# A recurrence on one core: output square sums with the next pair's, transposed values in the solve's first level, one convolution tap a half block later

## What is computed

```python
qkv_a = silu(causal_conv(qkv_a, conv_w))          # 4 taps per channel
q_a = l2norm(q_a) * (GDN_HEAD_DIM ** -0.5);  k_a = l2norm(k_a)
o_a = gated_delta_rule(q_a, k_a, v_a, g, beta)
o_a = rmsnorm(o_a, gdn_norm_w).reshape(b, s, GDN_WIDTH) * silu(z_a)

# gated_delta_rule, by chunks
l_mat = where(strict, einsum("bhncd,bhnjd->bhncj", k_beta, k) * decay, 0.0)
sol = triangular_solve(l_mat + eye, concatenate([v * beta, k_beta * exp(g_cum)], -1))
u, w = sol[..., :dv], sol[..., dv:]
def step(state, inp):
    v_new = u_c - w_c @ state
    o_c = q_c @ state + qk_c @ v_new
    return state * dec_c + k_c.T @ v_new, o_c
```

## Time and profile before

| | us |
|---|---|
| median of 3 runs | 3890.14 (3889.11 to 3890.8) |
| the profiled execution | 3890.46 |
| its span, first to last instruction | 3888.7 |
| TensorE busy | 3736.6 (96%) |
| its weight loads busy | 3492.0 (90%) |
| VectorE busy | 2862.1 (74%) |
| ScalarE busy | 1904.7 (49%) |
| mean granted TensorE clock | 0.993 of full speed |

### The profile page before, as it was taken

The page is one execution under the profiler, slowest core; times in us unless marked ns, Lnnn a source line. Parts: engine busy times, 40 slices in busy tenths (PEclk is TensorE's granted clock), DMA queues, the critical chain, the costliest instruction groups (busy, mean ns, idle before and its releaser), DMA issues.

```text
span 3888.7 us, 70287 instructions
## 1 busy us (share of the span) xinstructions
PE 3736.6 (96%) x27254; PEld 3492.0 (90%) x27254; DVE 2862.1 (74%) x3924; ACT 1904.7 (49%) x2898; POOL 186.9 (5%) x188
## 2 busy tenths in 40 slices
PE   1999999999999999999999999999999999999998
PEld 1999999899988999999989998999987888989888
DVE  8788887867779778888686776665676666666676
ACT  1556565435544355555534554454665433344365
POOL 0111111000000012121000000000000000000000
PEclk8999999999999999999999999999999999999999
DMA  9543443864468844434486445544534445455543
GB/s 394 182 145 142 141 145 135 302 236 164 155 239 317 290 148 141 150 135 151 146 317 214 158 152 182 185 163 172 190 120 149 177 181 188 180 184 184 184 143 128
DMA packets 138699, 720.49 MB, mean 185 GB/s; under 512 B 37696, under 2 KB 38144, under 8 KB 62336
## 3 DMA queue, kind: packets, MB, share of 16 engines
q1 hardware_dynamic: 111456, 631.31, 45.0%
q10 hardware_dynamic: 27040, 86.32, 6.6%
HBM read 711.22 MB, written 2.16 MB: 183 GB/s over the span
## 4 chain that ended last, share of the span: by engine, by line
PE 84%; DVE 7%; ACT 4%; issue 3%; DMA 2%; DVEq 0%; ACTq 0%; SPq 0%
PE bank L300 16%; PE bank L283 13%; PE bank L285 13%; PE bank L284 13%; PE bank L301 8%; PE bank L322 3%; PE bank L2410 2%; PE bank L2412 2%; PE bank L2411 2%; ACT Wh L356 2%; PE bank L326 2%; DMA raw<-in_ada 1%; DVE Wl L362 1%; PE bank L1077 1%; DVE gm_more L1308 1%
## 5 line engine op out<-in xcount | busy, mean ns | idle before, releaser
L356 ACT CAST Wh<-raw 128x1024 fp32r<-128x1024 f32 x1124 | 1168.2, 1047 | 1610.3 <-PE bank L285 913.5
L362 DVE TENSOR_TENSOR Wl<-raw,Wh 128x1024 fp32r<-128x1024 f32 x1124 | 1381.5, 1235 | 692.0 <-ACT Wh L356 688.9
L283 PE MATMUL bank<-H,Wh 128*128 128x256 f32 x4928 | 1445.5, 293 | 2.0 <-DVE Wl L362 1.2
L284 PE MATMUL bank<-H,Wh 128*128 128x256 f32 x4928 | 1393.0, 283 | 0.0
L285 PE MATMUL bank<-H,Wl 128*128 128x256 f32 x4928 | 1392.4, 283 | 0.0
L283 PEld LDWEIGHTS bank<-H,Wh 128*128 128x128 f32 x4928 | 941.6, 191 | 26.1 <-issue 13.6
L284 PEld LDWEIGHTS bank<-H,Wh 128*128 128x128 f32 x4928 | 942.2, 191 | 8.0 <-issue 4.8
L285 PEld LDWEIGHTS bank<-H,Wl 128*128 128x128 f32 x4928 | 941.3, 191 | 0.0
L300 PE MATMUL bank<-H,Wh 128*128 128x512 f32 x1792 | 631.8, 396 | 6.3 <-DVE WS L349 6.0
L301 PE MATMUL bank<-H,Wl 128*128 128x256 f32 x1792 | 502.6, 280 | 0.0
L300 PEld LDWEIGHTS bank<-H,Wh 128*128 128x128 f32 x1792 | 336.8, 188 | 89.3 <-issue 5.5
(11 more groups left out here) (413 smaller groups left out, 4481.8 us busy)
## 6 DMA issues: line engine op xcount, KB each, us to landing
raw<-in_stream SPq DMA_DIRECT2D x560, 1024.0 KB, 4.8
WS<-in_ada ACTq DMA_DIRECT2D x94, 512.0 KB, 6.3
raw<-in_ada SPq DMA_DIRECT2D x32, 1024.0 KB, 7.6
gm_more<-in_ada ACTq DMA_DIRECT2D x20, 512.0 KB, 7.5
WS<-rows_d ACTq DMA_DIRECT2D x16, 512.0 KB, 5.1
KR<-in_ada ACTq DMA_DIRECT2D x14, 512.0 KB, 6.9
raw<-in_stream SPq DMA_DIRECT2D x8, 512.0 KB, 7.0
gm_more<-WS ACTq DMA_DIRECT2D x32, 128.0 KB, 4.8
```

The costliest lines, as they stand in the source:

```text
L283: pe.matmul(out[:, 0:T], wh, xh[:, kt, :], start=first, stop=False)
L284: pe.matmul(out[:, 0:T], wh, xl[:, kt, :], start=False, stop=False)
L356: act.copy(Wh[:, n % 4, :], raw[:, (sbk + 2) % 4, k * (D // 2):(k + 1) * (D // 2)]).then_inc(hi_ready, 1)
L362: dve.tensor_tensor(Wl[:, n % 4, :], raw[:, (sbk + 2) % 4, k * (D // 2):(k + 1) * (D // 2)], Wh[:, n % 4, :].bitcast(F32), ALU.subtract).t ...
```

## The change

Four parts. (1) The transposition of the values moves from the middle of half 1 to the front of half 2, behind the first Z and turn. (2) ossq moves from the middle of half 11 into half 12, behind ssq of the next pair. (3) With it o_ln and o_rs, and the table load in front of them, move from ScalarE's step 12 to 13, o_out from VectorE's step 13 to 14, o_hi from ScalarE's step 14 to 15; o_lo stays at 15. (4) The second tap (tap 1) of convolution 1 moves on VectorE from step 6 to step 7.

```diff
--- before.py
+++ after.py
@@ -978,7 +978,7 @@
 
 
         LEVEL, SCAN, LEVELS, PACKED = 2, 8, 6, 5
-        TAPS = {4: ((0, (0, 1)),), 5: ((0, (2,)),), 6: ((0, (3,)), (1, (0, 1))), 7: ((1, (2, 3)),), 8: ((2, (0, 1, 2, 3)), (3, (0,))), 9: ((3, (1, 2, 3)),),
+        TAPS = {4: ((0, (0, 1)),), 5: ((0, (2,)),), 6: ((0, (3,)), (1, (0,))), 7: ((1, (1, 2, 3)),), 8: ((2, (0, 1, 2, 3)), (3, (0,))), 9: ((3, (1, 2, 3)),),
                 10: ((4, (0, 1)),), 11: ((4, (2, 3)),), 12: ((5, (0, 1)),), 13: ((5, (2, 3)),)}
         gates8 = ws(0, 8, T, of=gm_more)
 
@@ -1076,6 +1076,11 @@
                     S.wait(pe, "dve", f"t_of{s}", r)
                     S.done(pe.matmul(B[0][:, 0:T], n_pair if s == 32 else n_of, upper(Mm, s), start=True, stop=True), "pe", f"Z{s}")
                     S.done(pe.transpose(B[1][:, 0:P], t_of, ident), "pe", f"turn{s}")
+                if n == LEVEL:
+                    F.wait(pe, "dve", "silu_v", r)
+                    for u in range(4):
+                        m = pe.transpose(B[5][:, u * P:(u + 1) * P], unit(cs[:, 4:6, :], u), ident)
+                    S.done(m, "pe", "v_tok")
                 if n == LEVEL + PACKED:
                     S.wait(pe, "dve", "M64", r)
                     for u in range(4):
@@ -1094,11 +1099,6 @@
                     S.done(m, "pe", "WT")
 
             def middle(n):
-                if n == 1:
-                    F.wait(pe, "dve", "silu_v", r)
-                    for u in range(4):
-                        m = pe.transpose(B[5][:, u * P:(u + 1) * P], unit(cs[:, 4:6, :], u), ident)
-                    S.done(m, "pe", "v_tok")
                 if LEVEL <= n < LEVEL + PACKED:
                     s = 2 << (n - LEVEL)
                     S.wait(pe, "act", f"tt_of{s}", r)
@@ -1116,9 +1116,11 @@
                     state_value()
                 if n == SCAN + 2:
                     out_second()
-                if n == SCAN + 3:
-                    S.wait(pe, "act", "osq", r)
-                    S.done(pe.matmul(B[4][:, :], ones, osq, start=True, stop=True), "pe", "ossq")
+
+            def out_squares():
+
+                S.wait(pe, "act", "osq", r)
+                S.done(pe.matmul(B[4][:, :], ones, osq, start=True, stop=True), "pe", "ossq")
 
             def front(n):
                 if n == 1 and not chain:
@@ -1145,6 +1147,8 @@
             def after(n):
                 if fresh and chain and n > 1:
                     front(n)
+                if chain and n == SCAN + 4:
+                    out_squares()
 
             for n in range(16):
                 if chain:
@@ -1189,13 +1193,13 @@
                     S.wait(act, "pe", "o_second", r)
                     S.done(act.activation(osq, B[5][:, :].rearrange("p (a b) -> p a b", b=T), ACT.Square), "act", "osq")
                     S.done(act.copy(ot, B[5][:, :].rearrange("p (a b) -> p a b", b=T)), "act", "ot")
-                if n == SCAN + 4:
+                if n == SCAN + 5:
                     act_table(act, LN_EXP)
                     S.wait(act, "pe", "ossq", r)
                     S.done(act.activation(osq, B[4][:, :].rearrange("p (a b) -> p a b", b=T), ACT.Ln, scale=1.0 / P, bias=const("eps")), "act", "o_ln")
                     S.wait(act, "act", "o_ln", r)
                     S.done(act.activation(osq, osq, ACT.Exp, scale=-0.5, bias=const("zero")), "act", "o_rs")
-                if n == SCAN + 6:
+                if n == SCAN + 7:
                     S.wait(act, "dve", "o_out", r)
                     S.done(act.copy(Oh[:, bass.ds(c * 2, 2), :], ot), "act", "o_hi")
 
@@ -1390,7 +1394,7 @@
                 if n == SCAN + 7:
                     S.wait(dve, "act", "o_hi", r)
                     S.done(dve.tensor_tensor(Ol[:, bass.ds(c * 2, 2), :], ot, Oh[:, bass.ds(c * 2, 2), :].bitcast(F32), ALU.subtract), "dve", "o_lo")
-                if n == SCAN + 5:
+                if n == SCAN + 6:
                     S.wait(dve, "act", "o_rs", r)
                     S.wait(dve, "dve", "o_z", r)
                     S.done(dve.tensor_tensor(ot, ot, osq, ALU.mult), "dve", "o_out")
```

## The result

| | before | after |
|---|---|---|
| median of the runs, us | 3889.96 (3889.11 to 3890.8, 4 runs) | 3950.35 (3948.4 to 3951.45, 4 runs) |
| ratio | 1 | 1.0151, 95% interval 1.0139 to 1.0163 |
| the profiled execution, us | 3890.46 | 3948.4 |
| its span, us | 3888.7 | 3946.6 |
| mean granted clock | 0.993 | 0.989 |

The change makes the kernel 60 us slower, 1.5%.

A forecast was written before the change was run, and what follows sets the result against it. TensorE, busy 99 of 100 us in the recurrence, was taken as the bound. From 3890.46 us, stalls +52.2, ZT64 −7.7 and ossq −0.8 gave 3934.2; the clock's +16 gave 3950, range 3916 to 3968.

The forecast's parts named there:

- No slack at gram: TensorE at the gram matmuls: gram starts 0.14 us after qkn's end, so every delay of qkn's chain stalls TensorE.
- The cast of half 12: ScalarE's cast waits for half 12 on TensorE, which was to end 0.56 us later, at 307.13.
- The wait at ssq: TensorE, reaching ssq 1.32 us sooner, was to wait about 0.9 us there for VectorE's second sq_lo.
- The chain behind it: On ScalarE, table load, o_ln and o_rs follow the cast of half 12, shifting the key norm by 3.13 us.
- Gram: Gram on TensorE was to come 3.73 us later per pair, with TensorE about 3.0 us idle.
- The tap: Moving the convolution tap on VectorE was to remove TensorE's 0.55 us wait before ZT64, 7.7 us in all.
- The values: The four transposes on TensorE were to cost 0.43 us at either place: 0 change, at most 1.4 us from merging.
- The clock: TensorE's clock was to drop after the stall in 10 of 14 pairs, 1.6 us each: 16 us, ends 0 and 22.
- The sum: Whole run: stalls +52.2, ZT64 −7.7, ossq's wait in each layer's last pair −0.8, clock +16: 3950 us.
- the table load did not run early: Rival on ScalarE: the load runs while the cast waits, hiding 1.29 us per pair; 3916 us, chance 0.13.
- Gram is bound by qkn: Rival at TensorE's wait for qkn claimed gram is not really bound: 3889.8 us, or 3876 with sq_lo unbound; chance 0.08.
- the stall would come without any drop of the clock: Rival at TensorE's stall before gram: the stall alone, with no slower clock, giving 3934.2 us; chance 0.22.

The follow-up runs named there:

- squares alone: The changed kernel with the tap and the transposed values as before, so only the output-square part moved: 3962.69 us, ratio 1.0176 to the kernel before.

## Why the prediction was right

Step by step, in the order of the prediction, with after's numbers counted from osq (299.57 before in the same pair, 304.15 after):

- **No slack at gram.** Right to within 0.1 us. Gram's matmul came 1.36 us after qkn's start in the earlier trace rows; where it truly waits it comes 1.28 after (322.02 to 323.30), so 0.08 were to spare there. Its weight load had nothing to spare: it stands 0.15 behind its predecessor instead of 0.12, and 1.27 behind qkn's start (313.69), in all 14 pairs, and 1.27 is the distance in every kernel here in which gram waits for qkn. So qkn already held up this load before the change, by some 0.03 us, and the equal distances were not chance. The loads around gram in the kernel before:

```profile
314.81 0.19 PEld L285 LDWEIGHTS bank<-H,Wl 128*128 128x128 f32 x1
314.96 0.19 PEld L1064 LDWEIGHTS bank<-Y 128*128 128x128 f32 x1
```

- **The cast of half 12.** Expected 0.56 us after the end that half 12 had before: half 12 ended at 306.57, 7.00 after osq; the cast starts 7.61 after osq now, some 0.05 of it the release. 0.56, as worked out. The wait at ssq, read off VectorE's sq_lo, was 0.96 per pair, where I had said 0.9, and taking most of it away brought 0.88.
- **The chain behind it.** From the cast to the key norm I had 3.67 us (307.18 to 310.85); it is 311.76 to 315.47, 3.71. The key norm comes 3.17 us later from osq than before (8.15 to 11.32), against 3.13.
- **Gram.** 3.73 us later was expected; it is 304.15 to 323.30, 19.15, against 15.48 before: 3.67. The idle time is 2.94, against about 3.0.
- **The tap.** 0.55 us a pair expected, 0.52 measured alone.
- **The values.** 0, and 0 measured; the 1.4 us set down for merging did not come.
- **The clock.** 1.6 us per drop; the two lengths of a pair, 67.34 and 65.76, differ by 1.58. The number of pairs was the weak term: 10 of 14 by interpolation between two rows, 8 in the profiled execution. Interpolation by length is not a law: the same idle time of 2.94 to 2.97 us was followed by a drop behind 8, 13 and 4 of 14 grams in three kernels. The term came out near by luck as much as by reading, and its share of the uncertainty, 0 to 22 us, was rightly kept in the range.
- **The sum.** Pairs: 14 × (65.76 − 62.50) = 45.6, plus 8 × 1.58 = 12.6, together 58.2 us, against 56.8 between the first and the eighth grams (some pairs before were longer than 62.50). I had 14 × 3.73 − 7.7 = 44.5 and 16. The 0.8 us for the last pair of each layer were not measured apart. That 3950 and the measured 3950.35 agree to under 1 us is luck: the term of the clock was 3.4 us too high, and the runs of this kernel alone spread over 3 us.

The rivals: the table load did not run early. ScalarE had 3.24 us of idle time and still began the load only behind the cast; the Trainium skill's statement of first-in first-out queues (TensorE: Matmul & The Clock Gate, "Architectural detail") agrees with that row. A drain behind the load does not show either: o_ln starts 1.30 us after the load's start. Gram is bound by qkn in all 14 pairs after, and its weight load was before. That the stall would come without any drop of the clock holds for 6 of 14 pairs here, and for all where the stall was halved.

## What to carry to other kernels

Moving a step on an engine that is half idle is not free by itself: here an instruction placed *behind* a waiting one inherited that wait, and an idle time that was being used was lost. Look for the instruction that waits, list what stands behind it on its queue, and follow that list to the engine that bounds the kernel. And look for what is almost late, not only for what is late: a wait of zero does not stand in any list, but the distance from a producer to its consumer, equal in all repetitions and the same as where the consumer truly waits, shows it. For matmuls it is read at the weight loads.

## What the runs showed of the hardware

The clock fell at shorter idle times of TensorE than the 3.30 us of the earlier trace rows: at idle times of 2.94 to 2.97 us in 25 of 42 cases (8, 13 and 4 of 14 in three kernels, one profiled execution each), at 1.53 in none of 14 and at 0.16 and 0.28 in none. The stretch at 1.2 GHz began between 0.8 us ahead of gram and 1.3 us behind it. What decides between two stalls of the same length is not settled here. In the changed kernel each drop cost a pair some 1.6 us, so that it adds about half of the stall again; in squares alone it was 1.3 to 2.0.
